# mLSTM scan: where SyncE issues the load of the values within an output step

## The reference

```python
log_w = b_end[..., None] - b + ic
c_new = decay[..., None, None] * c_mat + jnp.einsum('bhs,bhsd,bhsv->bhdv', w, kc, vc)
s = jnp.einsum('bhtd,bhsd->bhts', qc, kc) * jnp.exp(log_d - m_t[..., None])
num = jnp.einsum('bhts,bhsv->bhtv', s, vc) + w_inter[..., None] * jnp.einsum('bhtd,bhdv->bhtv', qc, c_mat)
den = jnp.abs(jnp.sum(s, axis=-1) + w_inter * jnp.einsum('bhtd,bhd->bht', qc, n_vec))
h = num / jnp.maximum(den, jnp.exp(-m_t))[..., None]
```

```python
y_m = merge_heads_rms(hm_f + flip_t(hm_b), ml_norm, h.dtype) * jax.nn.sigmoid(o_m)
y_g = merge_heads_rms(og_f + flip_t(og_b), gla_norm, h.dtype) * jax.nn.silu(r_g)
y = jax.nn.sigmoid(mg_m) * (y_m @ w_proj_m) + jax.nn.sigmoid(mg_g) * (y_g @ w_proj_g)
```

## Time and profile before

| | |
|---|---|
| median of 3 runs | 2556.09 us (2553.77 to 2559.91) |
| the profiled execution | 2554.94 us |
| its span | 2552.5 us |
| the mLSTM scan in it | about 642 to 990 us |
| TensorE busy in those 348 us | 302.36 us, mean granted clock 0.94 |
| ScalarE, GpSimd, VectorE busy there | 123.67, 174.29 and 102.65 us |
| share of the 16 DMA engines there | 0.53 |

### The profile page before, as it was taken

One profiled execution on the slowest core, in us unless ns is written; L12 is line 12 of the kernel. 1 busy time (PEld: TensorE's weight loads), 2 busy tenths in 40 slices (PEclk: granted clock), 3 DMA queues, 4 the chain that ended last, 5 costly groups with the idle time before them and its releaser, 6 DMA issues. The chain is left out here.

```text
span 2552.5 us, 26920 instructions
## 1 busy us (share of the span) xinstructions
PE 2208.2 (87%) x10382; PEld 1790.1 (70%) x10382; DVE 1419.9 (56%) x1721; ACT 1009.7 (40%) x1263; POOL 861.3 (34%) x629
## 2 busy tenths in 40 slices
PE   6979979993787896799999949899748999999992
PEld 1268868883676785588888838778647788887882
DVE  0536452103332332688888635544247899998993
ACT  1412211111232443345555334432225667666662
POOL 5300001110344654366776521220003344443441
PEclk9989989996898997799999969999958999999996
DMA  7633244112453565243344366563337975559525
GB/s 272 236 74 94 80 144 145 50 46 96 153 177 112 157 171 180 73 122 120 118 130 116 92 207 204 160 218 113 102 133 304 364 274 158 156 158 333 169 58 164
DMA packets 262522, 397.63 MB, mean 156 GB/s; under 512 B 26934, under 2 KB 186806, under 8 KB 255612
## 3 DMA queue, kind: packets, MB, share of 16 engines
q1 hardware_dynamic: 232556, 242.26, 29.9%
q0 software_dynamic: 28112, 148.41, 18.5%
q10 hardware_dynamic: 1728, 5.25, 0.6%
HBM read 401.55 MB, written 88.67 MB: 192 GB/s over the span
## 5 line engine op out<-in xcount | busy, mean ns | idle before, releaser
L2573 DVE TENSOR_TENSOR ex_w_lo<-ex_raw,ex_w_hi 128x2048 fp32r<-128x2048 f32 x186 | 416.1, 2285 | 39.3 <-ACT ex_w_hi L2547 38.7
L2547 ACT ACTIVATE ex_w_hi<-ex_raw 128x2048 fp32r<-128x2048 f32 x182 | 337.7, 1909 | 173.4 <-DMA ex_raw<-in_w_up_dram,w_rows 84.2
L670 POOL DMA_DIRECT2D vals<-rows_stage x40 | 22.7, 567 | 437.5 <-ACT rows_stage L662 437.5
L882 PE MATMUL ml_u_ps<-half_hi,ml_u_w_hi 128*128 128x512 f32 x256 | 109.2, 426 | 26.7 <-ACT ml_u_exp L900 26.7
L2449 POOL DMA_INDIRECT ex_raw<-in_w_up_dram,w_rows x60 | 79.7, 1329 | 134.7 <-DVE ex_w_lo L2573 122.9
L1988 DVE TENSOR_TENSOR mo_w_lo<-mo_w,mo_w_hi 128x1024 fp32r<-128x1024 f32 x48 | 59.8, 1246 | 102.7 <-ACT mo_w_hi L1885 102.6
L1523 PEld LDWEIGHTS gl_lv_ps<-gl_q_level,gl_k_level 128*128 128x128 f32 x896 | 108.3, 194 | 10.2 <-issue 5.4
L2449 POOL DMA_INDIRECT ex_raw<-in_w_down_dram,w_rows x30 | 52.6, 1755 | 182.9 <-DVE ex_w_lo L2573 176.6
L882 PE MATMUL gl_u_ps<-half_hi,gl_u_w_hi 128*128 128x512 f32 x256 | 110.0, 430 | 3.2 <-ACT gl_u_exp L900 3.2
L1523 PE MATMUL gl_lv_ps<-gl_q_level,gl_k_level 128*128 128x64 f32 x896 | 111.0, 277 | 2.0 <-DVE gl_scores L1653 1.4
L2099 PE MATMUL mo_ps<-mo_branch_hi,mo_w_hi 128*128 128x512 f32 x256 | 106.4, 415 | 6.3 <-DVE mo_w_lo L1988 5.9
(11 more groups left out here) (397 smaller groups left out, 6157.3 us busy)
## 6 DMA issues: line engine op xcount, KB each, us to landing
fr_w<-in_w_mod_dram SPq DMA_DIRECT2D x12, 2048.0 KB, 9.9
ml_u_w<-in_w_in_dram SPq DMA_DIRECT2D x32, 512.0 KB, 6.1
gl_u_w<-in_w_in_dram SPq DMA_DIRECT2D x32, 512.0 KB, 5.2
vals<-rows_stage POOLq DMA_DIRECT2D x40, 256.0 KB, 2.3
ml_v<-vals SPq DMA_DIRECT2D x20, 512.0 KB, 4.4
gl_v<-vals SPq DMA_DIRECT2D x20, 512.0 KB, 3.4
qk_w<-in_w_in_dram SPq DMA_DIRECT2D x16, 512.0 KB, 4.6
rows_w<-in_w_in_dram SPq DMA_DIRECT2D x8, 1024.0 KB, 6.6
```

The costliest lines, as they stand in the source:

```text
L882: pe.matmul(self.ps[:, :], a_hi, b_hi, start=(k == 0), stop=False)
L2547: act.activation(hi[:, q, h], raw[:, q, h], ACT.Copy).then_inc(hi_done[q], 1)
L2573: dve.tensor_tensor(lo[:, q, at], raw[:, q, at], hi[:, q, at].bitcast(F32), ALU.subtract)\
```

## The change

Output steps (`n >= 0`) issue the load of the values of step u+2 last, behind the store of unit 2n-1 and, in a first visit, behind the store of the step's rows. Context steps (`n < 0`) keep the old place. No instruction is added or taken away, and every wait stays with its instruction.

```diff
                 if FIRST_OUT + 2 <= u + 2 < STEPS:
                     load_rows(u + 2)
-                if u + 2 < STEPS:
+                if u + 2 < STEPS and n < 0:
                     load_v(u + 2)
                 if n >= 1:
                     units.store(sp, 2 * n - 1)
                 if n >= 0 and first_visit(u):
                     store_h(u)
+                if u + 2 < STEPS and n >= 0:
+                    load_v(u + 2)
             units.store(sp, UNITS - 2)
             units.store(sp, UNITS - 1)
             units.all_stored(sp)
```

## The result

| | before | after |
|---|---|---|
| median | 2554.93 us (4 runs, 2553.46 to 2559.91) | 2529.16 us (4 runs, 2527.01 to 2533.64) |
| ratio | | 0.9898, 95% interval 0.9881 to 0.9916 |
| profiled execution, span | 2554.94, 2552.5 us | 2530.84, 2529.1 us |

The account below looks back on a forecast made before the run. TensorE's stalls in the eight silu units, behind late gate-row stores, were taken as the bound; some 19.0 us of stall and 7.6 of clock make 26.6 us, so 2530 us from a median of about 2556, range 2523 to 2541.

Parts of the forecast that it names:

- The bound: Silu units 8 to 15: ready odd gate store held 5.3 us in SyncE's wait for the last state product; TensorE loses 26.7 us.
- The new T: ScalarE's take of an odd silu unit: ended by TensorE's product, 7.08 us after the even take, 8.53 at slow clock.
- E: ScalarE's take of an even silu unit out of PSUM, still waiting for the even store; small TensorE stalls there grow.
- The store's landing: Odd gate store, issue to landing: 5.13 us before, bounds 2.0 and 5.1, taken as 2.0 to 2.3.
- Rival A: Odd store keeps landing in about 5.1 us; total 2539 us; chance 0.21 shared with Rival B.
- T to E: Time from an odd silu take to the next even one: stays at 14.08, 12.52 and 12.68 us.
- Rival B: Even stores land 1.5 us later, giving back 4.5 over three; total 2534 us; chance 0.21 shared with Rival A.
- The stalls: TensorE idle at even silu takes after the change: 3.0, 1.4 and 1.6 us, the 5 us ones gone.
- The one before unit 9: TensorE's first stall in the silu units, counted as 1.7 us after the change.
- The clock: TensorE units after stalls: one slow unit counted (1.45 us lost); some 7.6 us gained; 2.9 less if two more slow.
- The sum: mLSTM scan: 24.5 us gained step by step plus 2.1 for unit 16 at full clock, 26.6 in all.
- Rival C: A late row-store wait delays values and next weights, reaching TensorE in steps without silu units; about 2562 us; chance 0.03.

Follow-up runs that it names:

- t1: Against the kernel before, only the gate-row store of unit 2n-1 goes ahead of the values' load, the row store stays behind it; ratio 0.9901.
- t2: Against the kernel before, only the store of the step's rows goes ahead of the values' load, the gate-row store stays behind it; ratio 0.9989.
- t3: Against the kernel before, the new order in output steps n = 4 to 7 alone, the other ten keeping the old order; ratio 0.9885.
- t4: The changed kernel run again, nothing altered; ratio to the kernel before 0.9905.
- t12: The changed kernel with two fills on GpSimd at the mLSTM scan's end that delay the next stage; span 2522.9 us.
- t6: The kernel before, order kept, with four buffers instead of two for the mLSTM scan's gate rows; ratio 0.9858.
- t5: The changed kernel with the even store (unit 2n-2) ahead of the second weight load (unit 2n+3); 2516.38 us, ratio to the kernel before 0.9858.
- t7: The changed kernel with the values' load moved into the next step, behind its weight loads, even store and rows; ratio to the kernel before 0.9915.

## Why the prediction was right

**The bound.** It named the odd store held in a wait that wasn't its own, and t1, t2 and t3 show just this.

**The new T.** E + 7.08 was forecast; 749.32 to 756.39 is 7.07, and 7.08 and 7.10 in the later two; the slow one took 8.62 (770.48 to 779.10), and 8.53 was forecast. TensorE's product, not the store, ends it. The store's landing was the term bounded from far: 2.0 or 5.1 us. The take at 798.67 came 2.40 us after the store's issue at 796.27 (the unit before: 3.95 from 775.15), so it lands in 2.40 or less with the row store 0.36 us behind it. Rival A is out. The Trainium skill (DMA: Bandwidth & Descriptors, Anatomy of one DMA) fits its sum of 2.0 us plus the bytes at 436 GB/s to transfers that GpSimd issues, which the prediction didn't say. For this store, which SyncE issues, the estimate of 2.6 us made from it was too long by 0.2 or more.

**E.** T to E was carried over unchanged, 14.08, 12.52 and 12.68; measured 14.09, 12.49 and 12.51. Rival B didn't come: the even stores landed after 6.2, 4.6 and 4.6 us. The stalls were forecast as 3.0, 1.4 and 1.6 and measured as 3.24, 1.65 and 1.67. The one before unit 9, forecast at 1.7, is gone, which no step of mine had foreseen. In this execution TensorE came to that place later (unit 7 was taken at 738.70 instead of 737.06), but that is not the whole: the stall is missing in t4 too, where unit 7 was taken as early in the scan as before (95.2 us after its start in both). Unit 6's store landed after 4.7 to 4.8 us in the change's three profiles (with t4 and t12), after 5.9 to 7.0 in four profiles of the kernel before, and after 6.5 in t3, which keeps the old order at that point and still has a stall of 1.47 there. With the row store alone moved (t2) it took 4.8 and there was no stall, with the gate store alone (t1) 5.5 and 0.47. So the new order of the earlier steps hastens unit 8's take, and the row store's place seems to do the larger part of it; how it does so stays open.

**The clock.** One slow unit behind the 3 us stall (0.76, 7.19 us) and full clock behind the two shorter (1.00 in both): as forecast. It need not have come so. In t12 the stall at the same place was 3.15 us, and the unit behind it ran at 1.00. The Trainium skill (TensorE: Matmul & The Clock Gate, HAM oscillation), read as a rule for every idle gap, would have made all three slow; the rows disagree with that reading, which is wider than the page's own, since the page ties the fall to waits past a certain length.

**The sum.** 26.6 us forecast for the scan; 26.6 by its length in the first pair, and 26.3 between the means of four and two profiles (346.6 and 320.3). The medians moved by 25.8, from 2554.93 to 2529.16, where 2530 was forecast. The agreement to a us owes something to luck: single executions scatter by more (2527.01 to 2533.64), a stall that the sum had at 1.7 us didn't come, and the slow unit it counted (1.45 us) came in one execution and not in another.

**Rival C.** The row store went out 3.2, 4.5 and 2.9 us ahead of the values (754.02, 775.51, 796.63 against 757.26, 779.96, 799.54), against 3.2 to 4.7 forecast: the row store's wait never delayed them.

## What to carry to other kernels

In a queue that issues in program order, put each transfer by the time its wait ends, and look for stores that were ready while the queue sat in another wait: the interval from the producer's end to the issue shows it. A store counts as urgent when its buffer's next writer stands ahead of the critical engine; here a change worth 1% lay in four such places, and the even store, by the same test, held 9.5 us more. More buffers cure the same wait where memory allows (t6), so compare the two before choosing an order.

## What was not expected of the hardware

The same 256 KB store landed after 2.6 us in t5 though 1 MB had been issued 3.6 and 3.1 us before it (values at 755.25, weights at 755.82, store at 758.89). Right behind 512 KB (issued 0.4 us before it, in the changed kernel) it took 4.6 to 6.2. By their own landings, 3.8 and 5.0 us after the issue, the values were still under way for 0.2 us and the weights for 1.9 us when the store was issued. So the bytes issued ahead don't give a store's landing by themselves; how long ago they were issued goes with it. No run varies that alone.

What a short stall does to the clock can't be read from its length. In t7 a stall of 1.73 us left the clock full for the next unit, while one of 1.86 in the same execution was followed by 0.77. In the kernel before, 2.30 us were followed by 0.78, and in its fourth profile 2.51 us by 1.00. In the changed kernel, 3.24 us were followed by 0.76, and in t12 3.15 us by 1.00.
